# An attention stage started 5.6 weight tiles sooner, with wider slots and its first two transposes side by side

## The chip, the cores and the metric

One core of one Trainium2 chip runs the kernel. The metric is the device time of one execution in microseconds (us), as the median of several runs. Before the change it is 1154.45 us (three runs, 1153.80 to 1155.62).

## What is computed

A block of 512 tokens of width 1024, all in fp32, goes through two blocks of layers. What matters here is three attentions; the rest is matrix products with weights that are read once.

```
first_block:   x = rglru_layer(x)                      # two gemms around a recurrent scan
               k, v = rmsnorm(x) @ w_kv
               q, gate = rmsnorm(x) @ w_in
               o = sliding_window_sink_attention(q,k,v) # 16 heads of 64, blocks of 128 queries,
                                                        # one or two blocks of 128 keys
               x = x + (o * silu(gate)) @ w_out
second_block:  windowed_gqa (8 heads, 2 or 3 key blocks), neighborhood_attn (8 heads),
               gates, projections, an MLP of width 4096, a last norm
```

In the sink attention every row of scores gets a bias by distance, a maximum that also takes in a sink value, an exponential, a sum with the sink's share, a division, and a product with v.

## The kernel before

**The gemms.** All weights come as one stream of 1448 tiles of 128 x 128 (`ch.tiles`), in units of eight (`UT`). A unit is fetched to `raw`, rounded to `wh` on ScalarE (ACT, L892), and its remainder `wl` is made on VectorE (DVE, L1178), each as one 128x1024 instruction. A tile is three matmuls of 512 columns on TensorE (PE): high weights by high data (L693), high by low (L694), low by high (L695).

**One clock for all queues.** Each engine's program is written by `merge`: every lane of work is a generator that yields the tick at which its next instructions are due, and the lanes are merged by tick, the earlier lane first where ticks are equal. A tick is one weight tile of the stream. So a tick fixes only an instruction's place in its engine's queue; when it runs is then set by the queue before it and by its semaphore waits. The engines run their queues strictly in this order.

**The attentions.** `SETS` gives each attention its jobs, its first tick, and a step: "s" (the sink attention) jobs 0 to 15, "w" (the windowed one) jobs 16 to 23, "n" (the neighbourhood one) jobs 24 to 31. A job is four heads and one block of 128 queries; `nk` is its number of key blocks (1 or 2 in "s", 2 or 3 in "w", 2 in "n"). `plan_steps` lays the jobs out in slots. In slot n, of `wide` ticks, PE does at the slot's start the products with v of job n-2 (L860, `prods`), then the scores of job n (L817), and further on in the slot the transposes of job n-1 (L829, `turns`), four per key block, into one of two PSUM banks by turns. `wide` is the step times the number of items: four for the scores and one for each key block turned or multiplied.

**The chain of a job in "s".** Scores of four heads (PE L817); for each head, a bias and a minimum (DVE L1384), an exponential (ACT L1057); for each pair of heads, a sum with the sink on DVE (L1408), an exponential of it (ACT L1063), a sum and a reciprocal (DVE L1413, L1416), then two divisions on GpSimd (POOL L1638). Then in the next slot the transposes (PE L829), a copy out of PSUM of each key block, by DVE for an even one (L1430) and by ACT for an odd one (L1074), half a tick after the transposes' tick, and in the slot after that the products (PE L860). After every second job ACT copies the result out (L1084); DVE multiplies it by the gate (L1353, `y_mix`), ACT rounds it (L1045) and DVE makes the remainder (L1358) for the output gemm "wb". DVE takes the bias of heads 2 and 3 only after the reciprocal of heads 0 and 1, as all of it is one lane.

**Around "s".** The query gemm "bq" runs from tick 344 to 472. The first scores need the fifth normed chunk (`qn_done` 5, DVE L1324). Between the attention's instructions lie, in the same queues, the evictions of the gemm (DVE L1240 and L1347, ACT L1039), the norms of the heads (PE L765, ACT L1019, L1025, L1027, DVE L1324) and the weights' splitting. The output gemm "wb" starts at tick 472: twelve tiles on the first four chunks of `y2h`, and then tiles 484 to 487 on the chunks 4 to 7, which come from jobs 8 to 15.

The places that the constants give, in ticks (A_END is 328, B_END 536):

| | first scores | last scores | last transposes | last products | "n" starts |
|---|---|---|---|---|---|
| "s" before | 380.6 | 459.0 | 465.8, 466.6 | 467.9 | |
| "w" before | 586.3 | 655.8 and 661.3 | 668.3, 669.6 | 671.7 | 681.3 |

Of the kernel before, what the change touches and what calls it, by code (L numbers as in the profile page):

```python
# [186 lines left out]
def build(nc, xT, wst, par, cst, nbias, out):  # L187
    ctx = ExitStack()
    with ctx:
# [158 lines left out]
        A_END = end["wa", 7] + 1  # L348
        B_X = end["bq", 15] + 1
        B_END = end["wb", 7] + 1  # L350
# [58 lines left out]
        for m, job in enumerate(jobs):  # L409
            first = {"s": 0, "w": 16, "n": 24}[job["kind"]]  # L410
            job["no"], job["first"], job["t0"] = m, first, t_no
            t_no += job["nk"]
        SETS = {"s": (0, 16, A_END + 52.6, 0.74), "w": (16, 24, B_END + 50.3, 1.22), "n": (24, 32, B_END + 145.3, 1.6)}

        def head(job, i):

# [2 lines left out]
        def plan_steps(kind):  # L419


            a, z, tick, step = SETS[kind]
            at = {}
            for n in range(a, z + 2):
                n_prod = jobs[n - 2]["nk"] if n >= a + 2 else 0
                n_turn = jobs[n - 1]["nk"] if a < n <= z else 0
                wide = step * ((4 if n < z else 0) + n_turn + n_prod)
                for kb in range(n_prod):
                    at["prod", n - 2, kb] = tick
                for i in range(4 if n < z else 0):  # L430
                    at["score", n, i] = tick + (0.5 * wide if kind == "w" and i > 1 else 0.0)
                for kb in range(n_turn):
                    at["turn", n - 1, kb] = tick + wide * (0.3 + (0.0, 0.27, 0.4)[kb])
                tick += wide
            return at

        step_at = {}
        for kind in SETS:
            step_at.update(plan_steps(kind))
# [8 lines left out]

        att_end = {k: max(t for w, t in step_at.items() if SETS[k][0] <= w[1] < SETS[k][1]) for k in SETS}

# [148 lines left out]
        def _(e):  # L599
# [188 lines left out]
            def scores(kind):  # L788

                for m in range(*SETS[kind][:2]):  # L790
                    job = jobs[m]
# [27 lines left out]
            def turns(kind):  # L819
                for m in range(*SETS[kind][:2]):  # L820
                    job = jobs[m]
                    for kb in range(job["nk"]):
                        yield step_at["turn", m, kb]
                        t = job["t0"] + kb
                        q.wait_ge(pta_done if t % 2 else ptd_done, t // 2)
                        q.wait_ge(v_done, {"s": 1, "w": 2, "n": 2}[kind])
                        for i in range(4):
                            q.wait_ge(nrm_done, 4 * m + i + 1)
                            done = e.transpose(bank[TB[t % 2]][:, blk(i)], p_tile(m, i)[0][:, blk(kb)], ident)  # L829
                        done.then_inc(turn_done, 1)  # L830

            def prods(kind):
                for m in range(*SETS[kind][:2]):
                    job = jobs[m]
# [977 lines left out]
```

## Time and profile before

| | |
|---|---|
| median of the runs | 1154.45 us |
| the profiled execution's own time | 1155.51 us |
| its span, first to last instruction | 1153.7 us |
| PE busy | 1130.5 us, 98% |
| DVE busy | 637.5 us, 55% |
| ACT busy | 519.3 us, 45% |
| POOL busy | 159.0 us, 14% |
| mean granted TensorE clock | 0.996 |

1.8 us of the profiled execution lie outside its span. In a row of the timeline the first number is the start, the second how long the merged instructions take, and in brackets stands how long the engine sat idle ahead of it and who released it. Matmuls overlap, so distances between starts say more than durations.

### The profile page before, as it was taken

Reading aid. Unit: us, or ns where it says so; the run is one execution under the profiler, and the core shown is the slowest. Engines: PE = TensorE matmul, PEld = TensorE weight load, DVE = VectorE, ACT = ScalarE, POOL = GpSimd, SP = SyncE. Lnnn points to the kernel's source line nnn. Section 1 sums busy time; section 2 is a strip of 40 time slices with the busy share of each in tenths; the row PEclk is TensorE's granted clock in tenths of the full one; section 3 lists DMA queues with packets and bytes.
Section 4 is the critical chain, followed back from the end, with each engine's and each line's share of the span. In section 5 each row is a group of like instructions: output and inputs, shape, how many; then the busy total and the mean of one; then the engine's idle time right before and its main releaser. Section 6 shows DMA issues by size and latency. Waiting matters only on the chain.

```text
span 1153.7 us, 14370 instructions
## 1 busy us (share of the span) xinstructions
PE 1130.5 (98%) x5342; PEld 889.1 (77%) x5342; DVE 637.5 (55%) x1083; ACT 519.3 (45%) x904; POOL 159.0 (14%) x198
## 2 busy tenths in 40 slices
PE   9999889999999999999999999999999999999997
PEld 6787667887666678867777778888888888888886
DVE  7787887854567665455545544555454232544232
ACT  6656656544566544244434433334443211443231
POOL 2022112310223212032202210012000000000021
PEclk9999999999999999999999999999999999999999
DMA  6323222332111123212223123323223223223312
GB/s 225 110 73 91 92 73 92 110 110 74 55 56 55 37 77 107 97 52 71 91 74 111 59 70 101 101 92 107 95 91 109 92 93 106 90 95 103 98 55 74
DMA packets 30806, 102.82 MB, mean 89 GB/s; under 512 B 3344, under 2 KB 5648, under 8 KB 30736
## 3 DMA queue, kind: packets, MB, share of 16 engines
q1 hardware_dynamic: 30304, 101.37, 27.0%
q8 instruction: 43, 0.70, 0.2%
q10 hardware_dynamic: 432, 0.52, 0.1%
q14 instruction: 27, 0.22, 0.1%
HBM read 99.78 MB, written 2.10 MB: 88 GB/s over the span
## 4 chain that ended last, share of the span: by engine, by line
PE 84%; DVE 9%; ACT 5%; issue 2%; DMA 1%; SPq 0%; DVEq 0%; ACTq 0%
PE ps L693 25%; PE ps L695 24%; PE ps L694 24%; PE ps L817 3%; PE ps L829 2%; PE ps L860 2%; DVE xs L1253 2%; DVE wl L1178 1%; DVE Pt L1384 1%; ACT wh L892 1%; ACT Pt L1057 1%; DVE sg L1269 1%; PE ps L854 1%; DVE cc L1285 1%; PE ps L765 1%
## 5 line engine op out<-in xcount | busy, mean ns | idle before, releaser
L693 PE MATMUL ps<-xgh,wh 128*128 128x512 f32 x848 | 348.8, 411 | 7.9 <-DVE wl L1178 6.9
L695 PE MATMUL ps<-xgh,wl 128*128 128x512 f32 x848 | 332.6, 392 | 0.0
L694 PE MATMUL ps<-xgl,wh 128*128 128x512 f32 x848 | 332.0, 392 | 0.0
L1178 DVE TENSOR_TENSOR wl<-raw,wh 128x1024 fp32r<-128x1024 f32 x180 | 229.5, 1277 | 133.7 <-ACT wh L892 131.9
L892 ACT ACTIVATE wh<-raw 128x1024 fp32r<-128x1024 f32 x180 | 188.5, 1049 | 129.6 <-PE ps L695 128.9
L693 PEld LDWEIGHTS ps<-xgh,wh 128*128 128x128 f32 x848 | 160.1, 189 | 59.0 <-issue 29.5
L695 PEld LDWEIGHTS ps<-xgh,wl 128*128 128x128 f32 x848 | 159.8, 188 | 34.4
L694 PEld LDWEIGHTS ps<-xgl,wh 128*128 128x128 f32 x848 | 160.3, 189 | 32.4 <-issue 3.4
L1638 POOL TENSOR_SCALAR Pt<-Pt,stat 128x256 f32<-128x256 f32 (+2 forms) x128 | 74.7, 596 | 296.4 <-DVE stat L1416 217.8
L1057 ACT ACTIVATE Pt<-Pt,stat 128x256 f32<-128x256 f32 (+2 forms) x128 | 64.7, 506 | 107.6 <-DVE stat L1388 42.2
L693 PE MATMUL ps<-fh,wh 128*128 128x512 f32 x240 | 93.5, 389 | 0.0
L694 PE MATMUL ps<-fl,wh 128*128 128x512 f32 x240 | 93.5, 389 | 0.0
L695 PE MATMUL ps<-fh,wl 128*128 128x512 f32 x240 | 93.4, 389 | 0.0
L1121 ACT ACTIVATE f<-rl 128x512 f32<-128x512 f32 x32 | 20.2, 631 | 96.0 <-DVE rl L1541 96.0
L1612 POOL TENSOR_SCALAR ssq<-sq 128x512 f32<-128x512 f32 x4 | 2.6, 651 | 416.1 <-ACT sq L1141 297.0
L1294 DVE TENSOR_TENSOR xt<-ps,xt 128x512 f32<-128x512 f32 x39 | 26.8, 687 | 52.5 <-PE ps L695 52.4
L695 PEld LDWEIGHTS ps<-fh,wl 128*128 128x128 f32 x240 | 45.1, 188 | 9.4
L694 PEld LDWEIGHTS ps<-fl,wh 128*128 128x128 f32 x240 | 45.1, 188 | 9.3
L693 PEld LDWEIGHTS ps<-fh,wh 128*128 128x128 f32 x240 | 45.0, 188 | 9.3
L1615 POOL TENSOR_TENSOR ssq<-ssq,sq 128x512 f32<-128x512 f32 x27 | 37.8, 1398 | 98.6 <-ACT sq L1007 67.2
L1546 DVE TENSOR_TENSOR fl<-f,fh 128x512 fp32r<-128x512 f32 x32 | 22.2, 693 | 40.5 <-ACT fh L1125 40.5
L1541 DVE SCALAR_TENSOR_TENSOR rl<-ps,rstd 128x512 f32<-128x512 f32 x32 | 22.1, 692 | 36.5 <-PE ps L695 36.5
(219 smaller groups left out, 1582.1 us busy)
## 6 DMA issues: line engine op xcount, KB each, us to landing
raw<-wst SPq DMA_DIRECT2D x180, 512.0 KB, 3.4
bst<-nbias SPq DMA_DIRECT2D x8, 256.0 KB, 4.1
xt<-xT SPq DMA_DIRECT2D x3, 512.0 KB, 7.7
outT<-ot SPq DMA_DIRECT2D x2, 384.0 KB, 2.5
outT<-ot SPq DMA_DIRECT2D x6, 128.0 KB, 2.0
raw<-wst SPq DMA_DIRECT2D x2, 256.0 KB, 4.0
cstt<-cst SPq DMA_DIRECT2D x1, 512.0 KB, 5.8
xt<-xT ACTq DMA_DIRECT2D x1, 256.0 KB, 3.6
```

Source lines behind the costliest of these rows:

```text
L693: e.matmul(o, high, a, start=(k == 0), stop=False)
L694: e.matmul(o, high, b, start=False, stop=False)
L695: e.matmul(o, low, a, start=False, stop=stop).then_inc(tile_done, 1)
L817: e.matmul(score_place(m, i + p), own, seen, start=True, stop=True).then_inc(score_done, 1)
L829: done = e.transpose(bank[TB[t % 2]][:, blk(i)], p_tile(m, i)[0][:, blk(kb)], ident)
L860: done = e.matmul(bank[PV][r, 256 * half:256 * half + 256], v[:, job["k0"] + kb, 64 * g:64 * g + 64], src.rearrange("p (c h t) -> p c h t" ...
L892: e.activation(wh_t[:, u % NHL, :], raw_t[:, u % NRAW, :], ACT.Copy).then_inc(hi_done, 1)
L1057: e.activation(pa, pa, ACT.Exp, scale=-1.0, bias=stat_(m, 0, i, i + 1), accum_out=stat_(m, 1, i, i + 1)).then_inc(exp_done, 1)
L1178: e.tensor_tensor(wl_t[:, u % NHL, :], raw_t[:, u % NRAW, :], f32(wh_t[:, u % NHL, :]), ALU.subtract).then_inc(lo_done, 1)
L1294: e.tensor_tensor(xt[:, j, :], bank[ch.bank[name]], xt[:, j, :], ALU.add).then_inc(ev_done, 1)
L1615: e.tensor_tensor(ssq, ssq, sq[(n0 + j) % 2], ALU.add).then_inc(sum_done, 1)
L1638: e.tensor_scalar(pm, pm, stat_(m, 3, i, i + 1), 1.0, ALU.mult, ALU.mult).then_inc(nrm_done, 1)
```

## The change

It changes numbers in the planner alone; every instruction stays, with its waits, and only places in the queues move. "s" starts at A_END + 47.0 in place of A_END + 52.6, with a step of 0.82 in place of 0.74. In "s" and "w" a slot that has scores is at least 5.5 steps wide. In all three attentions the transposes of the first two key blocks of a job get one common place at 0.42 of the slot (before 0.30 and 0.57), and a third one 0.66 (before 0.70); the copies follow half a tick later, as before.

```diff
-        SETS = {"s": (0, 16, A_END + 52.6, 0.74), "w": (16, 24, B_END + 50.3, 1.22), "n": (24, 32, B_END + 145.3, 1.6)}
+        SETS = {"s": (0, 16, A_END + 47.0, 0.82), "w": (16, 24, B_END + 50.3, 1.22), "n": (24, 32, B_END + 145.3, 1.6)}
...
-                wide = step * ((4 if n < z else 0) + n_turn + n_prod)
+                wide = step * max(5.5 if n < z and kind != "n" else 0, (4 if n < z else 0) + n_turn + n_prod)
...
-                    at["turn", n - 1, kb] = tick + wide * (0.3 + (0.0, 0.27, 0.4)[kb])
+                    at["turn", n - 1, kb] = tick + wide * (0.42, 0.42, 0.66)[kb]
```

## Rows read from the trace of the kernel before

**Rows 1.** Busy time by stretch (start:end, length, busy us and count, then clock)

```profile
160.00:180.00 20.00, 16.88 (x65) 12.68 (x65) 18.70 (x22) 10.54 (x14) 3.36 (x3) 0.83 0.25 79
...
288.00:412.00 124.00, 118.36 (x652) 81.64 (x651) 82.11 (x283) 76.63 (x220) 32.80 (x64) 1.00 0.16 52
...
445.00:517.00 72.00, 71.29 (x325) 54.69 (x324) 35.20 (x73) 27.27 (x54) 11.10 (x14) 1.00 0.25 81
517.00:605.00 88.00, 88.00 (x463) 63.06 (x462) 45.18 (x122) 36.88 (x88) 19.04 (x26) 1.00 0.24 78
```

**Rows 2.** Who PE waited for: us in total, times, longest

```profile
PE ps L860 <- ACT PT L1074: 3.5, 6, 0.9
...
PE ps L817 <- DVE stat L1384: 1.1, 2, 0.7
PE ps L829 <- POOL Pt L1638: 1.0, 2, 0.7
...
PE ps L817 <- DVE stat L1388: 0.7, 1, 0.7
```

**Rows 3.** Timeline of PE in "s": products with and without a wait

```profile
312.52 0.65 PE L860 MATMUL ps<-PT,V 128*64 128x256 f32 x4
314.05 0.65 PE L860 MATMUL ps<-PT,V 128*64 128x256 f32 x4 [0.87 <-ACT PT L1074]
...
321.81 1.08 PE L860 MATMUL ps<-PT,V 128*64 128x256 f32 x8
322.82 1.13 PE L817 MATMUL ps<-ke,q 64*128 64x256 f32 x8
323.89 0.50 PE L693 MATMUL ps<-xgh,wh 128*128 128x512 f32 x1
```

**Rows 4.** Timeline of PE around four transposes

```profile
302.63 0.39 PE L695 MATMUL ps<-xgh,wl 128*128 128x512 f32 x1
...
302.86 0.60 PE L829 MATMUL ps<-cstt,Pt 128*128 128x128 f32 x4
...
303.21 0.47 PE L693 MATMUL ps<-xgh,wh 128*128 128x512 f32 x1
...
303.53 0.39 PE L694 MATMUL ps<-xgl,wh 128*128 128x512 f32 x1
```

**Rows 5.** Timeline of DVE and ACT within two slots of "s"

```profile
302.20 0.48 DVE L1384 CUSTOM_DVE_ANT_0 Pt<-ps,cstt,drv 128x256 f32<-128x256 f32 x1 [0.95 <-PE ps L817]
...
304.62 0.48 DVE L1384 CUSTOM_DVE_ANT_0 Pt<-ps,cstt,drv 128x256 f32<-128x256 f32 x1
...
305.74 0.19 ACT L1063 ACTIVATE stat<-stat 128x2 f32<-128x2 f32 x1
...
327.40 0.69 DVE L1430 COPY PT<-ps 128x512 f32<-128x512 f32 x1
...
328.00 0.48 DVE L1384 CUSTOM_DVE_ANT_0 Pt<-ps,cstt,drv 128x256 f32<-128x256 f32 x1
...
330.36 0.58 ACT L1074 ACTIVATE PT<-ps 128x512 f32<-128x512 f32 x1
```

**Rows 6.** The page's groups of the weights' splitting

```profile
L1178 DVE TENSOR_TENSOR wl<-raw,wh 128x1024 fp32r<-128x1024 f32 x180 | 229.5, 1277 | 133.7 <-ACT wh L892 131.9
L892 ACT ACTIVATE wh<-raw 128x1024 fp32r<-128x1024 f32 x180 | 188.5, 1049 | 129.6 <-PE ps L695 128.9
```

**Rows 7.** Timeline where the first scores would stand

```profile
286.54 0.75 DVE L1324 SCALAR_TENSOR_TENSOR q<-q,drv,ps 128x512 f32<-128x512 f32 x1 [3.54 <-ACT ps L1027]
...
288.43 0.39 PE L693 MATMUL ps<-xgh,wh 128*128 128x512 f32 x1
```

**Rows 8.** Timeline from the last result of "s" to tile 484

```profile
410.08 0.60 ACT L1084 ACTIVATE q<-ps 128x512 f32<-128x512 f32 x1 [0.18 <-PE ps L860]
...
418.18 0.69 DVE L1358 TENSOR_TENSOR y2l<-sgt,y2h 128x512 fp32r<-128x512 f32 x1 [0.70 <-ACT y2h L1045]
...
420.98 0.39 PE L693 MATMUL ps<-y2h,wh 128*128 128x512 f32 x1
```

**Rows 9.** Timeline of PE after its longest idle time

```profile
169.06 0.77 PE L693 MATMUL ps<-xgh,wh 128*128 128x512 f32 x1 [3.12 <-DVE wl L1178]
...
170.05 0.63 PE L695 MATMUL ps<-xgh,wl 128*128 128x512 f32 x1
...
174.74 0.44 PE L694 MATMUL ps<-xgl,wh 128*128 128x512 f32 x1
```

## Prediction

> **What bounds the kernel now.** I read the page first: PE is busy 98% of the span, the others at most 55%. With PE as the bound and no instruction removed, the change can only move PE's idle time and what a different neighbour costs a matmul. So the second view is busy time by stretch. In "s" (288 to 412 us) PE is busy 118.36 of 124.00 us, so 5.6 us are idle; in the first part of "w" 0.7 us; in the rest of "w" and the start of "n" none [rows 1]. The third view, who PE waited for, names them: the products for an odd key block's copy on ACT, 3.5 us in six waits; the scores for a bias on DVE, 1.1 us and 0.7 us; the transposes for a division on POOL, 1.0 us [rows 2]. These add up to 6.3 us, all inside "s" and "w"; PE's other waits lie ahead of "s" or in the last norm, and the change doesn't touch them.
>
> A wait costs more than its idle time, since matmuls overlap. Eight products that run unbroken take 1.01 us to the next group, so four take 0.50; where the copy is late the second four start 1.53 after the first, so that wait cost 1.03 us where 0.87 is shown [rows 3]. With 0.16 more for each of the six, the sum is 6.3 + 1.0 = **7.3 us**. That is the most that better places can give back.
>
> **Why the products wait.** Count from the first bias of a job, B, in a slot with little else in it. The fourth bias starts at B + 2.42 and the second pair's sink exponential ends on ACT at B + 3.73 [rows 5]. Before, the even copy's place (slot start + 0.30 x 5.92 + 0.5 = 2.3 ticks) is between the third and the fourth bias (the latter at 2.5 ticks), and the row shows it there: the copy at 327.40 takes 0.69 and only then the fourth bias runs [rows 5]. That puts the ACT chain, and the odd copy queued behind it, 0.69 later: ready for the copy at B + 4.4, copied at B + 5.0 (0.58 each).
>
> When is it wanted? The scores end 0.14 ahead of B. A slot of 5.92 ticks holds 5.92 tiles of 0.69 us (three matmul distances of 0.23 [rows 4]) = 4.1, and two groups of transposes, 0.88 together. Products start at about B + 4.8, the odd block's 0.5 later: B + 5.3. The slack is 0.3 us. A slot also holds, about once per eight tiles, a weight split of 1.05 on ACT and 1.28 on DVE [rows 6]. With one of them in the chain a wait of 0.7 to 1.0 comes out, the size of the longest one read (0.9 [rows 2]).
>
> **The change, part by part.**
>
> *Width, 0.74 to 0.82.* A full slot becomes 8 x 0.82 = 6.56 ticks: 0.64 tiles more, 0.44 us of slack. Nothing is paid, for the tiles are the stream's own. The cover is that enough of them lie between ticks 375.0 and 473.4. What moves is the attention's length, from 87.3 to 98.4 ticks.
>
> *Transposes at 0.42 twice.* The common place is 2.76 ticks into the slot, so the copies stand at 3.26: behind the fourth bias (2.5) and its sum (2.7), ahead of the second pair's reciprocal (3.45). DVE then copies while it would wait for ACT. The ACT chain is free at B + 3.7, no longer at B + 4.4. Transposes start after three tiles, at about B + 1.9, and end by B + 2.8; both copies are done by about B + 3.8 (DVE) and B + 4.3 (ACT). Products start at B - 0.14 + 4.5 + 0.9 = B + 5.3, the odd block's at B + 5.8. Slack is 1.5 us where it was 0.3, or 1.2 more than before; the longest wait, 1.03, is below that. The other waits of "s" go the same way: transposes of a job stand 9.0, 7.8 and 7.4 ticks behind its scores (jobs 8, 9, 10) where they stood 7.4, 6.5 and 6.0, so 0.9 us or more is added to waits on POOL of at most 0.7 [rows 2]; job 1's scores stand 4.5 ticks behind job 0's, not 3.0, which is 1.0 us against 0.7 [rows 2].
>
> Of 6.6 us in "s" (7.3 less the 0.7 of "w") I leave 0.8 for slots in which two splits and an eviction meet the chain: **-5.8**. The ends are 0 and -6.6.
>
> *"w".* Its first slot grows from 4.88 to 6.71 ticks. The wait there (0.7) is job 17's first scores on job 16's biases; 2.5 ticks between them become 3.3, worth 0.55 us: **-0.5**. The last products move from tick 671.7 to 673.5 while "n" starts at 681.3 as before, so that costs nothing. The third transposes stand 2.9 ticks (2.0 us) after the first two, whose bank a copy of 0.69 must free. The "w" of before is 88 us without PE idle behind its first slots [rows 1], so nothing more can be won there; I put what can be lost at 0 to 1.
>
> *Side by side, as such.* Four transposes put 0.44 into a run of matmuls: from L695 to the second matmul behind is 0.90 against 0.46 [rows 4]. Three distances within the four are the 0.60 less one transpose's own latency; with the 0.39 of a wide matmul they would be 0.07, and at 0.11 the four alone make up the 0.44. In that case two groups together save nothing; the other end is that the slow step after the group (0.32 against 0.23 [rows 4]) is paid once per group, and 28 jobs (12, 8 and 8) save 0.09 each, 2.5 us. I take **0**, as four by 0.11 already explain the whole 0.44.
>
> *The start, 5.6 ticks sooner.* Scores at tick 375.0 tie with tile 375 and come behind it, so at 288.43. The fifth normed chunk is there at 286.54 + 0.75 = 287.29 [rows 7]: no wait, with 1.1 us to spare. Behind it DVE now holds the biases in front of the eviction of the value chunk (tick 376.2). That chunk's transposes (378.5) feed the copy of V on ACT (379.7), queued behind job 0's exponentials, and job 0's transposes at 381.4 need V. I count the copy done about when they are due: **+0.2**, between 0 and 1.
>
> *The end, 5.5 ticks later.* Last products go from 467.9 to 473.4. Before, the last remainder ends at 418.87 and tile 484, the first that needs the second half, starts at 420.98 [rows 8]: 2.1 us to spare. 5.5 ticks are 3.8 us, so moved as a whole the tail would be 1.7 us late. But tile 487, not 484, needs that last chunk, 2.0 us more, and the last chunk waits in part for its own gate (tick 474.6), which doesn't move. Counted from the result's copy: the end of copy at +0.7, then on DVE four mixes, four remainders and one split, 8 x 0.69 + 1.28 = 6.8, end at 7.5, against tile 487 at 10 + 3 tiles, 8.9. **0**, with 1.7 at the far end.
>
> Sum: -5.8 - 0.5 + 0.2 = **-6.1 us**. From the profiled span: 1153.7 to 1147.6, with the 1.8 outside it 1149.4. The profiled execution was 1.06 above the median, so the median goes from 1154.45 to **1148.3 us**.
>
> **A page's rule against it.** In the one place where PE sat idle for 3.12 us, matmuls afterwards start 0.43 apart (1.2 GHz in place of 2.4) up to 174.74, and the clock of that stretch is 0.83; in "s", with its groups of four transposes, it is 1.00 [rows 1, 9]. The Trainium skill (TensorE: Matmul & The Clock Gate, Part 4: PE-mode transpose) says that the full clock doesn't engage for transpose-mode work, which doesn't count as PE-busy the same way. By that, longer runs of transposes are a risk to the clock; groups of four show no trace of it.
>
> **The rivals.**
>
> *Waits only move (1151.8).* The chain wins its 1.2 us, but splits, evictions and head norms now meet it elsewhere, and each slot has 11% more of the stream's work beside it. Half of the 5.8 comes back. For it: DVE and ACT are busy 66% and 62% in "s" [rows 1]. Against: the longest wait read is below the slack won.
>
> *No change worth measuring (1153.5).* The waits are ACT's and DVE's own work time per job, which no place alters. Against: both are idle a third of "s".
>
> *Slower (about 1157): the even copy becomes late.* It moves from the third to the fifth place of a slot's DVE work; with a split (1.28), an eviction and a gate (0.69 each) ahead of it, it ends at B + 3.8 + 2.7 = B + 6.5 against products at B + 5.3. In 12 of 14 full slots that would be 14 us, less the 7.3; if it meets them in 7, +1. It decides from about 0.6 us per full slot on. Against: the three come once in eight tiles, rarely all ahead of the copy, and DVE is idle a third of the time.
>
> *The clock falls in runs of eight transposes (1151 and up).* A fall costs what it did above: 13 matmuls at 0.20 more, 2.6 us each time [rows 9].
>
> **How the numbers follow.** Forecast, a gain of 4 to 8.5: 0.68. Waits only move: 0.14. No change: 0.09. Slower: 0.07. Clock: 0.02. A measurement can tell 0.2%, 2.3 us, from no change. Faster takes the forecast and nearly all of the second case, 0.80; within 0.2% 0.13; slower 0.07. The range goes from 1145.9 (all 7.3 and part of the 2.5) to 1152.3, which takes in the second case.
>
> **What would show it.** The waits of L860 on L1074, L829 on L1638 and L817 on L1384 and L1388 all but gone; DVE's even copy behind the fourth bias; PE idle under 1.5 us in the stretch of "s"; transposes in eights adding 0.88; no PE idle ahead of tile 484; clock 1.00. I am wrong if L860 waits for L1430, if a wait appears at the first transposes or at the first tiles of "wb", or if "w", without idle time now, gets some.

## The result, and the profile after

The changed kernel takes 1150.30 us (median of 6 runs, 1149.57 to 1150.57) where the one before took 1154.68 on the same chip (6 runs, 1153.46 to 1156.0). The ratio is 0.9962, with a 95% interval of 0.9950 to 0.9974: 4.4 us faster, between 3.0 and 5.8. The forecast was 1148.3, a gain of 6.1.

By the page PE is the bound as before, busy 98% of the span.

The stretches that answer to [rows 1], with the same columns:

```profile
160.00:180.00 20.00, 17.61 (x75) 13.06 (x75) 18.87 (x22) 10.55 (x14) 3.38 (x3) 0.91 0.24 79
...
288.00:412.00 124.00, 119.81 (x665) 85.21 (x662) 84.75 (x285) 76.52 (x222) 35.25 (x64) 1.00 0.18 56
...
445.00:517.00 72.00, 72.00 (x331) 54.52 (x330) 35.56 (x75) 26.13 (x53) 9.58 (x14) 1.00 0.25 81
517.00:605.00 88.00, 87.78 (x462) 63.99 (x460) 46.01 (x127) 39.45 (x95) 20.23 (x27) 1.00 0.24 78
```

In "s" (288 to 412 us) 4.2 us of PE are idle where 5.6 were; "w" lost its 0.7 and has 0.2 elsewhere. The first line is the surprise: nothing was changed ahead of 288 us, yet it reads 0.91 where [rows 1] has 0.83. So two profiled spans are not compared as wholes here. The matmuls of line 732 (a norm's sum) stand at the same place of PE's queue ahead of "s", behind it and behind "n"; their starts cut the span into comparable stretches. Before, and then after:

```profile
255.00 1.02 PE L732 MATMUL ps<-ssq,cstt 128*128 128x512 f32 x2
...
461.78 1.02 PE L732 MATMUL ps<-ssq,cstt 128*128 128x512 f32 x2
...
800.22 1.02 PE L732 MATMUL ps<-ssq,cstt 128*128 128x512 f32 x2
```

```profile
254.05 1.02 PE L732 MATMUL ps<-ssq,cstt 128*128 128x512 f32 x2
...
457.67 1.02 PE L732 MATMUL ps<-ssq,cstt 128*128 128x512 f32 x2
...
795.30 1.02 PE L732 MATMUL ps<-ssq,cstt 128*128 128x512 f32 x2
```

"s" went from 206.78 to 203.62, **-3.16**; "w" with "n" from 338.44 to 337.63, **-0.81**. The 0.95 ahead of the first of them belongs to no edit. The second profiled execution of the changed kernel gives 203.62 and 337.61, so these two numbers repeat within 0.02. The kernel before and each version of the experiments were profiled once.

Who PE waited for after the change, to be held against [rows 2]:

```profile
PE ps L693 <- DVE wl L1178: 5.6, 3, 3.0
PE ps L860 <- ACT PT L1074: 3.0, 3, 1.2
...
PE ps L860 <- DVE PT L1430: 1.0, 3, 0.6
...
PE ps L785 <- DVE th L1469: 0.2, 1, 0.2
```

The waits of the transposes for POOL (1.0) and of the scores for a bias (1.1 and 0.7) are gone. The products' waits for the odd copy are three in place of six, but nearly as long together, and the longest is 1.2 where it was 0.9. Three waits for the even copy are new. PE's timeline shows the worst of each kind, and the eight transposes ahead of one:

```profile
339.93 0.39 PE L695 MATMUL ps<-xgh,wl 128*128 128x512 f32 x1
...
340.16 1.03 PE L829 MATMUL ps<-cstt,Pt 128*128 128x128 f32 x8
...
340.95 0.48 PE L693 MATMUL ps<-xgh,wh 128*128 128x512 f32 x1
...
341.27 0.40 PE L694 MATMUL ps<-xgl,wh 128*128 128x512 f32 x1
...
365.65 0.65 PE L860 MATMUL ps<-PT,V 128*64 128x256 f32 x4 [1.18 <-ACT PT L1074]
...
372.92 1.08 PE L860 MATMUL ps<-PT,V 128*64 128x256 f32 x8 [0.56 <-DVE PT L1430]
```

From L695 to the second matmul behind it the eight take 1.34 against 0.46: they add 0.88, exactly twice the 0.44 of four [rows 4]. What the odd copy (L1074) of these eight waits for is on ACT's own timeline:

```profile
341.79 1.28 ACT L1039 ACT_TABLE_LOAD   x1
343.08 0.63 ACT L1039 ACTIVATE th<-gu 128x512 f32<-128x512 f32 x1
343.62 0.49 ACT L1057 ACTIVATE Pt<-Pt,stat 128x256 f32<-128x256 f32 x1
344.20 0.57 ACT L1074 ACTIVATE PT<-ps 128x512 f32<-128x512 f32 x1
```

Its input was ready at 341.2; it starts at 344.20, behind a gate with its table load and behind the slot's fourth exponential. The products then wait 0.99 at 344.83.

The other two waits, 0.86 at 302.35 and the longest, 1.18 at 365.65, are of another kind, and the change made them. Jobs 1 and 9 have a single key block, which ACT copies, and it is turned in a slot of six items. Its place went from 0.30 to 0.42 of that slot, so the copy's went from 1.8 ticks (0.30 x 4.44 + 0.5) to 2.6 (0.42 x 4.92 + 0.5), past the third exponential (2.2). Job 9's copy and that exponential, before and then after:

```profile
365.33 0.57 ACT L1074 ACTIVATE PT<-ps 128x512 f32<-128x512 f32 x1
366.59 0.51 ACT L1057 ACTIVATE Pt<-Pt,stat 128x256 f32<-128x256 f32 x1 [0.68 <-DVE stat L1384]
```

```profile
364.00 0.51 ACT L1057 ACTIVATE Pt<-Pt,stat 128x256 f32<-128x256 f32 x1 [0.82 <-DVE stat L1384]
364.51 0.61 ACT L1045 ACTIVATE y2h<-sgt 128x512 fp32r<-128x512 f32 x1
365.03 0.57 ACT L1074 ACTIVATE PT<-ps 128x512 f32<-128x512 f32 x1
```

Before, no products waited for the copy of job 1 or 9. Now these two make 2.04 of the 3.0 us, and no table load stands ahead of either.

### The profile page after: what moved, and what is told of

Its sections match the earlier page's. It is cut to its first block, busy times and chain, and to the rows that moved or that the text cites. A ratio compares the mean times of both kernels' runs of the same rounds, so it can differ in the third digit from the quotient of the medians.

```text
span 1148.8 us, 14370 instructions
## 1 busy us (share of the span) xinstructions
PE 1129.4 (98%) x5342; PEld 890.7 (78%) x5342; DVE 638.4 (56%) x1083; ACT 518.6 (45%) x904; POOL 160.8 (14%) x198
## 4 chain that ended last, share of the span: by engine, by line
PE 83%; DVE 9%; ACT 5%; issue 2%; DMA 0%; SPq 0%; DVEq 0%; ACTq 0%
PE ps L693 25%; PE ps L695 24%; PE ps L694 24%; PE ps L817 3%; DVE xs L1253 2%; PE ps L829 2%; PE ps L860 2%; DVE wl L1178 2%; ACT Pt L1057 1%; PE ps L854 1%; PE ps L765 1%; ACT xs L939 1%; ACT wh L892 1%; DVE cc L1285 1%; DVE sg L1269 1%
## 5 line engine op out<-in xcount | busy, mean ns | idle before, releaser
L693 PE MATMUL ps<-xgh,wh 128*128 128x512 f32 x848 | 345.3, 407 | 6.0 <-DVE wl L1178 5.6
L695 PE MATMUL ps<-xgh,wl 128*128 128x512 f32 x848 | 332.2, 392 | 0.0
L695 PEld LDWEIGHTS ps<-xgh,wl 128*128 128x128 f32 x848 | 159.8, 188 | 34.3
L1638 POOL TENSOR_SCALAR Pt<-Pt,stat 128x256 f32<-128x256 f32 (+2 forms) x128 | 76.5, 610 | 293.0 <-DVE stat L1416 217.8
L695 PE MATMUL ps<-fh,wl 128*128 128x512 f32 x240 | 93.4, 389 | 0.0
L695 PEld LDWEIGHTS ps<-fh,wl 128*128 128x128 f32 x240 | 45.0, 188 | 9.3
```

The source lines that it names most:

```text
L693: e.matmul(o, high, a, start=(k == 0), stop=False)
L695: e.matmul(o, low, a, start=False, stop=stop).then_inc(tile_done, 1)
L1638: e.tensor_scalar(pm, pm, stat_(m, 3, i, i + 1), 1.0, ALU.mult, ALU.mult).then_inc(nrm_done, 1)
```

## Experiments

"Stretch s" below is the time from the first to the second start of line 732, beside the 206.78 of before. All diffs are against the changed kernel unless the kernel before is named. The first four ran together, then the next four, then the last four, each four with runs of the kernel before on the same chip (medians 1153.75, 1154.38 and 1154.39).

**1. The old places of the transposes.** One part undone:

```
-  at["turn", n - 1, kb] = tick + wide * (0.42, 0.42, 0.66)[kb]
+  at["turn", n - 1, kb] = tick + wide * (0.3 + (0.0, 0.27, 0.4)[kb])
```

> The changed kernel with the transposes' places as before (0.30, 0.57, 0.70 of the slot), so the sooner start, the step of 0.82 and the least width alone. Theory (slack in ticks is what ends the waits, and both parts give some): job 1's scores and the transposes no longer wait (0.8 and most of 1.5 us), the products gain 0.44 us per slot; a gain of 2 to 3.5 us, about 1152.0 us. Rival 1 (the start and width give all): 1150.3, as the changed kernel. Rival 2 (the common place gives all): 1154.7, as before.

Measured: 1150.64, ratio 0.9974 (0.9963 to 0.9986), stretch s 203.70, which is -3.08. The waits:

```profile
PE ps L860 <- ACT PT L1074: 1.7, 3, 0.9
...
PE ps L829 <- POOL Pt L1638: 1.5, 1, 1.5
```

By the stretch the whole gain of "s" is there without the common place; the ratio can't be told from the changed kernel's. With the transposes earlier the products wait less (1.7) and the transposes more (1.5). The products of jobs 1 and 9 don't wait, as their copies stand ahead of the third exponential again. No wait for the even copy shows; it stands ahead of the fourth bias as before.

**2. The new places alone**, on the kernel before: its L433 gets the fractions (0.42, 0.42, 0.66) and nothing else.

> The kernel before with the transposes at 0.42, 0.42, 0.66 alone. Theory: the transposes stand 0.7 ticks later behind their divisions and the odd copy is free sooner, but the even copy has only 0.58 of 5.92 ticks left until the products; a gain of 0.5 to 2.5 us, about 1153.0. Rival 1: 1154.7. Rival 2: 1150.3. If this is slower than before, the late even copy has a price that the width pays for.

Measured: 1153.36, ratio 0.9995 (0.9986 to 1.0004), so by the whole time no change can be told; stretch s -1.48, the next stretch +0.47.

```profile
PE ps L860 <- ACT PT L1074: 2.6, 3, 1.3
PE ps L860 <- DVE PT L1430: 2.6, 4, 1.4
```

The even copy behind the fourth bias is late in a slot of the old width: 2.6 us of waits where before had none. The next stretch gets a wait of 0.7 (L785 for L1469), and the scores' 0.7 and 0.7 stay. The transposes' waits for POOL are gone. The rival "the even copy becomes late" is real as a mechanism; with the wider slots 1.0 us of it is left.

**3. The attention three ticks later**, to see whether the start or the tail costs anything:

```
-  "s": (0, 16, A_END + 47.0, 0.82)
+  "s": (0, 16, A_END + 50.0, 0.82)
```

> The changed kernel with the attention started at A_END + 50.0, so that all of it stands 3.0 ticks later and its last products at 476.4. It measures the tail's margin: 3 ticks are 2.05 us, I count 1.4 us between the last remainder and tile 487, so a wait of 0.6 us or less at the first tiles of the output gemm, about 1150.8. If the tail moved as a whole against tile 484, it would be waiting already in the changed kernel and 2 us more here, 1152.4. At the start nothing changes, as no wait was there.

Measured: 1149.09, ratio 0.9958 (0.9946 to 0.9971), stretch s -4.26. The odd copy's waits stay at 3.0 us in three; those for the even copy are gone, and no PE idle time appears ahead of tile 487, where up to 0.6 was expected. A start sooner than this buys nothing.

**4. The odd copy sooner in ACT's queue**, in all three attentions. The transposes stay; the copy moves from half a tick behind them to the same tick. In full slots ACT then has it between the third and the fourth exponential, where it stood behind the fourth and the sink's:

```
 at L1070 (ACT)
-  yield step_at["turn", m, kb] + 0.5
+  yield step_at["turn", m, kb] + 0.0
```

> The changed kernel with ACT's copies half a tick sooner, at the transposes' own place, ahead of the fourth exponential of the slot. Theory (the odd copy is late because it is queued behind the fourth exponential, which itself hangs on DVE): the three waits of products on ACT, 3.0 us idle, go or shrink to under 1, and the median is about 1148.5. Rival (the wait only changes its cause: what is late is the even copy on DVE, or the exponentials held up behind the copy delay the next job): 1150.3 or more, with L860 waiting for L1430.

Measured: 1147.67, ratio 0.9947 (0.9934 to 0.9961), stretch s -5.38.

```profile
PE ps L860 <- DVE PT L1430: 0.9, 3, 0.6
...
PE ps L860 <- ACT PT L1074: 0.4, 1, 0.4
```

Job 1, in its slot of six items, where the copy passes the third exponential; first in the changed kernel, then here:

```profile
299.50 0.60 PE L829 MATMUL ps<-cstt,Pt 128*128 128x128 f32 x4
...
301.21 0.51 ACT L1057 ACTIVATE Pt<-Pt,stat 128x256 f32<-128x256 f32 x1 [0.82 <-DVE stat L1384]
...
301.72 0.58 ACT L1074 ACTIVATE PT<-ps 128x512 f32<-128x512 f32 x1
302.35 0.65 PE L860 MATMUL ps<-PT,V 128*64 128x256 f32 x4 [0.86 <-ACT PT L1074]
```

```profile
298.84 0.60 PE L829 MATMUL ps<-cstt,Pt 128*128 128x128 f32 x4
...
299.63 0.58 ACT L1074 ACTIVATE PT<-ps 128x512 f32<-128x512 f32 x1
...
300.54 0.51 ACT L1057 ACTIVATE Pt<-Pt,stat 128x256 f32<-128x256 f32 x1 [0.33 <-DVE stat L1384]
...
300.76 0.65 PE L860 MATMUL ps<-PT,V 128*64 128x256 f32 x4
```

Behind the exponential the copy also sits through ACT's 0.82 us of idling for a bias from DVE, with its own input long there; ahead of it, it is done 0.55 before the products start. Job 9's wait of 1.18 is gone in the same way. The 0.4 that is left stands at 341.6, where the gate with its table load is still ahead of the copy and only the fourth exponential is not: 0.42 in place of 0.99. This one place is worth 2.2 us of "s".

**5. The changed kernel once more**, as it is, on the chip of the next three.

> The changed kernel itself, beside the others of this chip: a ratio of about 0.996, 1149.4 if the kernel before takes 1153.8.

Measured: 1150.07, ratio 0.9960 (0.9947 to 0.9974).

**6. Experiments 3 and 4 together.**

> Both edits that did better than the changed kernel at once: ACT's copies at the transposes' own place, and the start at A_END + 50.0. Each took waits of products away: alone 6.1 and 4.7 us below the kernel before. If they take the same waits, this is as the ACT copies alone (1147.7); if the later start helps through other waits (DVE's copy, the first slots), 1147.0.

Measured: 1147.18, ratio 0.9936 (0.9924 to 0.9948), stretch s -6.49. Of PE's waits in "s" two are left, 0.7 of L860 for L1430 and 0.2 of L817 for L1384.

**7. The even copy ahead of the fourth bias again**, with everything else as changed:

```
 at L1426 (DVE)
-  yield step_at["turn", m, kb] + 0.5
+  yield step_at["turn", m, kb] + (-0.3 if kind == "s" else 0.5)
```

> The changed kernel with DVE's copies of the sink attention 0.8 ticks sooner, which puts them back ahead of the slot's fourth bias, as before the change. My prediction took it that the copy behind the fourth bias frees the ACT chain by 0.69 us. By that the waits of products on ACT grow: about 1151.5 (some 1 to 2 us more than the changed kernel). Rival (the place behind the fourth bias only trades waits on ACT for waits on DVE): the 1.0 us of waits on L1430 go and those on L1074 grow by as much, 1149.4 as the changed kernel.

Measured: 1152.34, ratio 0.9980 (0.9971 to 0.9989), stretch s -0.85.

```profile
PE ps L860 <- ACT PT L1074: 5.5, 6, 1.4
```

With the copy in front of the bias the odd copies come later: 5.5 us of waits for 3.0, and 2.3 us of "s". This is the step of the prediction about the even copy, tried by undoing it. It is not the 0.69 of the copy alone: the copy's place is now 0.3 ticks ahead of its own transposes', and DVE waits 1.7 us for transposes in two places where it waited 0.8 in one. Only with later transposes does it hold, though: in experiment 1 the same order cost nothing.

**8. The least width of 5.5 units only in "s".**

```
-  wide = step * max(5.5 if n < z and kind != "n" else 0, ...
+  wide = step * max(5.5 if n < z and kind == "s" else 0, ...
```

> The changed kernel with the least width of 5.5 steps in the sink attention alone, so that the windowed attention's first slot is 4.88 ticks again. Its one wait, 0.8 us ahead of job 17's scores, should be back: 0.5 to 0.8 us more than the changed kernel, about 1150.1. Rival: that wait comes from the transposes' place, then no difference.

Measured: 1151.61, ratio 0.9975 (0.9966 to 0.9984), against the 1150.07 of experiment 5. The intervals overlap, the runs hardly (the lowest here is 1150.70, the highest there 1150.79). One execution of the eleven took 6446 us and is left out of the ratio; it leaves the median as it is. The profile was of that one, so where the 1.5 us lie is not shown. Other profiles put less on this edit: from the second to the third start of line 732 ("w" with "n") experiment 1, with the width and without the common place, takes 337.81 (457.18 to 794.99), and experiment 11, with neither, 338.40 (459.02 to 797.42). That is 0.6 us.

**9. Six ticks later**, `A_END + 53.0`.

> The changed kernel with the attention started at A_END + 53.0, all of it 6.0 ticks later, its last products at 479.4. The run at + 50.0 had no wait at the output gemm and fewer waits of products by chance of what they meet. Here the products end 4.6 tiles before tile 484, so 3.2 us, and the result's copy, four mixes and four remainders need 7.5 by my count against tile 487: a wait of about 2 us at tiles 484 to 487, 1151 to 1152. If there is none, my count of the tail is wrong.

Measured: 1152.13, ratio 0.9978 (0.9969 to 0.9988), stretch s -1.22. Now the tail comes late for the second half's first tiles:

```profile
422.15 0.47 PE L693 MATMUL ps<-y2h,wh 128*128 128x512 f32 x1 [0.81 <-DVE y2l L1358]
```

With one of 0.27 and one of 0.26 ahead of it this makes 1.3 us, and two more kinds come back (0.6 of L817 for L1384, 0.4 of L829 for L1638). The 0.6 is that of job 1's scores, at 297.81, though the least width is there. This start is 0.4 ticks later than before the change, and yet the waits of "s" outside the tail are 4.1 us (2.8, 0.6, 0.4 and 0.3) beside 4.0 in the changed kernel. So the sooner start is what keeps the tail clear, and not what shortens the waits of the chain as a whole.

**10. The copy as in experiment 4 and step 0.86.**

> The changed kernel with ACT's copies at the transposes' own place and a step of 0.86, so that the last products stand at about 478. If slack is still what the remaining waits (1.3 us) need, they go and 1147.0 comes out; if the tail takes it, 1148 to 1149 with waits at tiles 484 to 487.

Measured: 1147.13, ratio 0.9936 (0.9924 to 0.9949), stretch s -6.59. With experiment 6 this is the best version, faster than both kernels; the two can't be told apart. The tail begins to show: the output gemm waits 0.3 for L1045, at 414.07.

**11. Step 0.82 alone**, on the kernel before, whose start and places stay.

> The kernel before with the step of 0.82 alone, started at A_END + 52.6 as before, so its last products stand at 477.4. If the wider slots give the gain and the sooner start only makes room for them, this gains what the run without the new places of the transposes did in the sink attention (about 2.5 us), less what the tail now costs: 1151.5 to 1153. If the sooner start itself gives something, about 1154.

Measured: 1152.73, ratio 0.9987 (0.9978 to 0.9996), stretch s -1.60, the next -0.04.

```profile
PE ps L817 <- DVE stat L1384: 0.7, 1, 0.7
PE ps L817 <- DVE stat L1388: 0.7, 1, 0.7
```

The odd copy's waits (2.9) and the transposes' (0.9) are little less; the first scores' waits of 0.7 and 0.7 are untouched, so the step isn't what removes them. In "w" that leaves the least width, the one other edit of its first slots. In "s" the least width alone doesn't do it: experiment 9 has it and job 1's scores wait 0.6 there.

**12. The odd copy sooner, on the kernel before**, in "s" alone, from half a tick behind the transposes to 0.6 ahead of that tick, which in full slots is again between the third and the fourth exponential:

```
 at L1070 (ACT), kernel before
-  yield step_at["turn", m, kb] + 0.5
+  yield step_at["turn", m, kb] + (-0.6 if kind == "s" else 0.5)
```

> The kernel before with ACT's copies of the sink attention 1.1 ticks sooner (0.6 ahead of their transposes' place), so ahead of the fourth exponential of the slot, as in the run that did best. There the odd transposes come later (0.57 of the slot), so ACT stands before them with the exponentials queued behind. If the gain of that edit needs the common place of the transposes, this gains under 1.5 us (1153 to 1155); if the copy's place alone does it, 3 us or more (1151).

Measured: 1152.35, ratio 0.9982 (0.9973 to 0.9991), stretch s -1.92.

```profile
PE ps L817 <- DVE stat L1384: 2.3, 3, 1.2
...
PE ps L860 <- ACT PT L1074: 0.4, 1, 0.4
```

Here too the odd copy's waits go (3.5 to 0.4), but in slots of the old width the next job's scores wait in their place. So 3.1 us of waits taken away give 1.9. The copy's place is worth -1.92 here and -2.2 on top of the change, so it adds to the other edits. The transposes' common place doesn't: -1.48 alone (experiment 2), -0.1 on top of width and start (experiment 1 against the changed kernel). There it takes 1.5 us of waits from the transposes, and the products' waits rise from 1.7 to 4.0.

The early start alone, with the old step, wasn't tried: job 8's scores would come ahead of the ninth normed chunk that they read.

## Why the prediction was right, and where its sum was off

Direction and range held, and the mechanism in part: waits of "s" and "w" went, at no price, but of the 4.5 us that the products' waits for the odd copy cost by the prediction's count, only 0.8 came back. The gain is 4.4 where 6.1 were forecast, and nearly all of the difference lies in one term. That the time came out inside the forecast's own span, a gain of 4 to 8.5, is partly luck: it is 0.4 from its edge, and in "s" the rival by which half of 5.8 comes back (-2.9) is nearer to the measured -3.16 than the forecast.

- *"7.3 us, the most that better places can give back"*, 6.6 of it in "s": too small. The two best versions gain 6.49 and 6.59 in "s" with 0.9 and 1.0 us of waits still in it. The sum adds 0.16 of overlap to each of the products' waits and nothing to the others. Before the change, four transposes with a wait of 0.65 for POOL at 363.38 take 2.01 from L695 (362.11) to the second matmul behind (364.12), against the unbroken 0.90 [rows 4]: 1.11 for 0.65.
- *"Of 6.6 us in "s" I leave 0.8 for slots in which two splits and an eviction meet the chain: -5.8"*: the step that was mis-sized. It measured -3.16, so 3.4 stayed in place of 0.8. In my own breakdown of that stretch by what stands between the tiles, the transposes give 1.5, job 1's scores 0.8 and all products and scores behind them only 0.8. Two things were missed. The slack of 1.2 was counted in a slot of eight items, with two key blocks to turn. In the six-item slots of jobs 1 and 9 the new fraction put the odd copy behind the third exponential, and 2.04 of the 3.0 us of waits for it are new there. And in the full slot the count has an ACT that is free at B + 3.7; at 344.20 a gate with its table load (1.28 + 0.63) and the fourth exponential stand ahead of the copy, which starts 3 us after its input: 0.99. The waits became fewer and longer, not none. Experiment 4, which lets the copy pass an exponential, returns 2.2 of the missing 2.6, and takes away both new waits.
- *The even copy behind the fourth bias*: with the new transposes' place the copy ahead of it does cost (experiment 7, 2.3 us), but it was wrong as the source of the gain: experiment 1 has the old order and the old fractions, and the same stretch s within 0.1. What gained is the wider slot, with the start that makes room for it.
- *Width, "0.44 us of slack"*: the step alone gives 1.6 of the 3.1 (experiment 11). By difference from experiment 1, the rest, about 1.5, comes from the first slots' least width and the start together. No run has one of these two alone; experiment 9 shows nearly as little waiting outside the tail with a late start.
- *"Nothing is paid" for the width*: right; experiment 10 goes to 0.86 and still gains.
- *Other waits of "s" (POOL, the first scores)*: right, gone.
- *"w", -0.5*: -0.81. Most of it is the 0.7 that was named. A wait of 0.2 appeared for L1469 at 559.56, in a stretch that had none. Experiment 8 puts this edit at 1.5 us by medians alone, the profiles of experiments 1 and 11 at 0.6; which of the two is nearer stays open.
- *Side by side as such, 0*: right; 0.88 for eight, so joining groups saves nothing of the matmuls' time, and the far end of -2.5 didn't come.
- *The start, +0.2*: 0; no wait of the first transposes (L829) shows. PE's rows show the first scores unhindered, and DVE's the chunk that they need, 1.2 us before (1.1 were counted against [rows 7]):

```profile
285.60 0.75 DVE L1324 SCALAR_TENSOR_TENSOR q<-q,drv,ps 128x512 f32<-128x512 f32 x1 [3.53 <-ACT ps L1027]
...
287.57 0.72 PE L817 MATMUL ps<-ke,q 64*128 64x128 f32 x8
```

- *The tail, 0*: right, by the count given. The result's copy starts at 410.05; the last remainders end at 417.36, 7.3 later (7.5 counted), and tile 487 starts at 418.90, so 1.5 us are to spare (1.4 counted). Tile 484 itself, at 416.86, doesn't need them, as said; to be held against [rows 8]:

```profile
410.05 0.60 ACT L1084 ACTIVATE q<-ps 128x512 f32<-128x512 f32 x1 [0.90 <-PE ps L860]
...
415.88 1.48 DVE L1358 TENSOR_TENSOR y2l<-sgt,y2h 128x512 fp32r<-128x512 f32 x2
...
416.86 0.39 PE L693 MATMUL ps<-y2h,wh 128*128 128x512 f32 x1
...
418.90 0.39 PE L693 MATMUL ps<-y2h,wh 128*128 128x512 f32 x1
```

Experiment 3 asks for three ticks more, 2.1 us at 0.69 a tick, but counted from the first start of line 732 its result's copy comes only 0.6 later (409.97 less 253.34, against 410.05 less 254.05), inside the margin of 1.5: no wait. In experiment 9 it comes 3.7 later (415.14 less 255.44), 2.2 beyond the margin, and PE is idle for 1.3.

- *The rivals.* "Waits only move" was nearly right for "s": near half of the 5.8 did stay, 3.0 us as waits on ACT, two of the three at places that had none, and 1.0 us as the even copy's. Its time of 1151.8 is a slip: with half of 5.8 back, 1148.3 becomes 1151.2. "The even copy becomes late" is in the trace too, three times with 0.56 at most. Its form is the one that was described, DVE with an eviction between the third and the fourth bias, and then the copy. (Its price was counted over "14 full slots"; by the plan nine slots have eight items.)

```profile
370.58 0.46 DVE L1384 CUSTOM_DVE_ANT_0 Pt<-ps,cstt,drv 128x256 f32<-128x256 f32 x1
370.98 0.69 DVE L1240 TENSOR_TENSOR gu<-ps,rstd 128x512 f32<-128x512 f32 x1
371.58 0.47 DVE L1384 CUSTOM_DVE_ANT_0 Pt<-ps,cstt,drv 128x256 f32<-128x256 f32 x1
...
372.17 0.69 DVE L1430 COPY PT<-ps 128x512 f32<-128x512 f32 x1
```

- *The clock.* With runs of eight transposes, "s", "w" and the start of "n" read 1.00, the level of 2.4 GHz, and the matmul behind the eight takes 0.48 and the next 0.40, as behind four. The risk that was drawn from the Trainium skill (TensorE: Matmul & The Clock Gate, Part 4: PE-mode transpose) didn't show at this length of run.

Of the signs named in advance, "L860 on L1074 all but gone" and "PE idle under 1.5 us" came out false, with 4.2. Of the signs of being wrong two came true in small: L860 waits for L1430 (1.0), and "w" got a wait (0.2). The first three point at the same term.

## What to carry to other kernels

A copy that PE waits for belongs in its engine's in-order queue right where its input comes ready, not behind work that is needed later; look at what stands ahead of it (here exponentials that themselves wait for DVE, and once a gate with its table load) before counting slack from averages. Look in every kind of slot: a place given as a fraction of the slot moved two copies past an exponential in the narrower slots, where nobody had counted. Edits that meet the same waits are not to be summed (the common place was worth 1.5 us alone and 0.1 on top of the wider slot), while one that takes work out from ahead of the copy kept its worth on either kernel. When waits are to vanish through slack, allow for the longest run of foreign work that can stand ahead in the queue, and expect fewer and longer waits rather than none.

## What the runs showed of the hardware

Ahead of 285 us all these kernels issue the same work, yet their profiles differ. In the thirteen profiles of executions of the usual length PE sits idle for a weight's remainder twice for long. Near 125 us it is 3.02 to 3.08 us in all of them, and still the granted clock of 120 to 140 us reads 1.00 before, 0.91 after and 0.83 in experiment 4. Near 169 us it is 3.12 with a clock of 0.83 in 160 to 180 us before [rows 1, 9], 2.39 with 0.91 after, and 1.51 with 1.00 in experiment 4, whose row of that stretch is:

```profile
160.00:180.00 20.00, 18.49 (x86) 13.75 (x85) 18.87 (x22) 10.43 (x14) 3.27 (x3) 1.00 0.23 79
```

So the same idle time was followed by a fall of the clock in one execution and by none in another. At 169 us too the length alone doesn't tell: experiment 11 has 3.12 with 0.91, experiment 10 2.28 with 1.00. What else decides is not shown here. The first start of line 732 lies anywhere from 253.34 to 255.44 in these profiles, 2.1 us that no edit made and that are half of what was to be measured.

The execution of 6446 us is the one that experiment 8's profile shows. Its matmuls of 512 columns take 1.69 to 1.76 us on average where those of before take 0.39 to 0.41, PE is busy for 6436 us, and the granted clock reads 1.00 in all of it. DVE and ACT are busy for 633 and 523 us, about as before. So TensorE was slow, and the clock's row doesn't show it; why stays open.
